# A gated scan on TensorE: small matmul groups joined across heads

## The reference, cut to what matters

```python
A = einsum('bhtd,bhsd,bhtsd->bhts', qc, kc, exp(b_t - b_s))   # t >= s
o = einsum('bhts,bhsv->bhtv', A, vc) + einsum('bhtd,bhdv->bhtv', qc * exp(b), S)
S = exp(b_last) * S + einsum('bhsd,bhsv->bhdv', kc * exp(b_last - b), vc)
```

## Time and profile before

| | |
|---|---|
| median of three runs | 1440.71 us |
| the profiled execution | 1440.95 us |
| its span | 1439.2 us |
| TensorE busy | 1422.2 us, 99% |
| VectorE busy | 873.3 us, 61% |
| ScalarE busy | 573.9 us, 40% |

### The profile page before, as it was taken

One profiled execution on the slowest core, in us unless ns is written; L12 is line 12 of the kernel. 1 busy time (PEld: TensorE's weight loads), 2 busy tenths in 40 slices (PEclk: granted clock), 3 DMA queues, 4 the chain that ended last, 5 costly groups with the idle time before them and its releaser, 6 DMA issues.

```text
span 1439.2 us, 20231 instructions
## 1 busy us (share of the span) xinstructions
PE 1422.2 (99%) x8048; PEld 1176.2 (82%) x8048; DVE 873.3 (61%) x1720; ACT 573.9 (40%) x1076; POOL 0.2 (0%) x4
## 2 busy tenths in 40 slices
PE   8999999999999999999999999999999999999998
PEld 6888888888888888888888888888787787787786
DVE  8887776543333335756467434423788888888655
ACT  6423345423232324533232333423455454555441
POOL 0000000000000000000000000000000000000000
PEclk9999999999999999999999999999999999999999
DMA  9656441352222224023232323222222222222221
GB/s 344 221 197 238 150 158 46 126 198 101 91 100 103 88 102 147 30 103 103 88 103 88 109 97 118 87 89 88 74 74 74 74 74 74 74 74 74 74 73 59
DMA packets 43726, 157.88 MB, mean 110 GB/s; under 512 B 4849, under 2 KB 5233, under 8 KB 43633
## 3 DMA queue, kind: packets, MB, share of 16 engines
q1 hardware_dynamic: 43344, 156.39, 30.9%
q10 hardware_dynamic: 288, 0.21, 0.0%
HBM read 154.48 MB, written 2.10 MB: 109 GB/s over the span
## 4 chain that ended last, share of the span: by engine, by line
PE 97%; DVE 2%; ACT 1%; issue 0%; DMA 0%; ACTq 0%; DVEq 0%
PE PS L503 30%; PE PS L505 29%; PE PS L504 29%; PE PS L898 1%; PE PS L499 1%; PE PS L902 1%; PE PS L892 1%; PE PS L653 1%; PE PS L917 1%; PE PS L844 0%; PE PS L878 0%; PE PS L857 0%; DMA CST<-in_cst 0%; PE PS L886 0%; PE PS L868 0%
## 5 line engine op out<-in xcount | busy, mean ns | idle before, releaser
L503 PE MATMUL PS<-HH,WH 128*128 128x512 f32 (+1 forms) x1072 | 424.1, 396 | 0.0
L505 PE MATMUL PS<-HH,WL 128*128 128x512 f32 (+1 forms) x1072 | 412.0, 384 | 0.0
L504 PE MATMUL PS<-HL,WH 128*128 128x512 f32 (+1 forms) x1072 | 411.3, 384 | 0.0
L1049 DVE TENSOR_TENSOR WL<-RAW,WH 128x1024 fp32r<-128x1024 f32 x217 | 263.9, 1220 | 70.9 <-ACT WH L1765 70.6
L1765 ACT ACTIVATE WH<-RAW 128x1024 fp32r<-128x1024 f32 x217 | 228.7, 1056 | 168.4 <-PE PS L505 133.6
L505 PEld LDWEIGHTS PS<-HH,WL 128*128 128x128 f32 x1072 | 201.5, 188 | 41.2
L503 PEld LDWEIGHTS PS<-HH,WH 128*128 128x128 f32 x1072 | 201.7, 188 | 37.3
L504 PEld LDWEIGHTS PS<-HL,WH 128*128 128x128 f32 x1072 | 202.0, 188 | 35.7
L503 PE MATMUL PS<-WH,ZH 128*128 128x512 f32 x400 | 155.9, 390 | 0.0
L504 PE MATMUL PS<-WL,ZH 128*128 128x512 f32 x400 | 155.7, 389 | 0.0
L505 PE MATMUL PS<-WH,ZL 128*128 128x512 f32 x400 | 155.7, 389 | 0.0
(11 more groups left out here) (268 smaller groups left out, 1758.6 us busy)
## 6 DMA issues: line engine op xcount, KB each, us to landing
RAW<-in_w_fc SPq DMA_DIRECT2D x64, 512.0 KB, 3.2
RAW<-in_hgrn_in SPq DMA_DIRECT2D x64, 512.0 KB, 3.2
RAW<-in_ada SPq DMA_DIRECT2D x44, 512.0 KB, 4.4
RAW<-in_pool_in SPq DMA_DIRECT2D x40, 512.0 KB, 3.3
RAW<-in_w_in SPq DMA_DIRECT2D x26, 512.0 KB, 5.1
RAW<-in_pool_out SPq DMA_DIRECT2D x16, 512.0 KB, 3.2
RAW<-in_hgrn_out SPq DMA_DIRECT2D x16, 512.0 KB, 3.2
RAW<-in_w_out SPq DMA_DIRECT2D x8, 512.0 KB, 3.7
```

Source lines behind the costliest of these rows:

```text
L503: e.matmul(out, wh, xh, start=first, stop=False)
L504: e.matmul(out, wh, xl, start=False, stop=False)
L505: return e.matmul(out, wl, xh, start=False, stop=last)
L1049: e.tensor_tensor(lo, raw(i), hi.bitcast(F32), ALU.subtract).then_inc(taken.sem, taken(i))
```

## The change

- mixing takes two heads: m, the head before, and o, the one before that (heads 0 to 12; LATE = 13 and on finish within their own time). For m: levels 0, 8 and 16 as one group (small_levels), then level 32. For o: level 64 directly behind that group, the turned keys directly behind m's level 32 in the same bank (columns 0 to 383, level 32 in 384 to 447), states, outputs.
- Level 64 is made of 8 matmuls with 32 stationary columns, no longer 4 with 64.
- The steps at which side work goes on are given for each engine. TensorE: 2, 6, 10, 13; VectorE: 2, 9, 11, 18; ScalarE: 3, 7, 8, 13; longer lists for heads 14, 15 and 16. The norm transposes (turn) have steps of their own on TensorE (1, 6, 7, 10) and VectorE (1, 7, 8, 12).
- The gate product of VectorE is at step 1 of the next head (3 before); head 15's at its own step 23.
- At the start keep_going(14) is keep_going(9), and first_low(0) stands ahead of first_modulation(1, 8).

```diff
-            if h == 15 and L in (16, 32, 64, "kt"):
-                return {16: 3, 32: 4, 64: 3, "kt": 4}[L]
-            return {0: 3, 8: 4, 16: 7, 32: 3, 64: 4, "kt": 7, "ds": 3}[L]
+            if h == 15:
+                return {16: 5, 32: 3, 64: 4, "kt": 3, "ds": 4}[L]
+            return {16: 7, 32: 5, 64: 5 if h < LATE else 7, "kt": 5 if h < LATE else 7, "ds": 4}[L]
+        def turned(h):
+            return (copied.sem, copied.of("kt", h)) if h < LATE else banks.taken(("kt", h))
+        def old(h):
+            return h - 2 if 2 <= h <= LATE + 1 else None
...
-            keep_going(14)
+            keep_going(9)
...
                 k0, q1 = halves(t.k, 32)[0], halves(t.q, 32)[1]
                 for i in range(8):
-                    r, c = 32 * (i % 4), 32 * (i // 4)
+                    r, c = 32 * (i % 4), 384 + 32 * (i // 4)
                     m = e.matmul(PS[b][r:r + 32, c:c + 32], k0[:, i, :], q1[:, i, :], start=True, stop=True)
+                if keys is not None:
+                    e.wait_ge(scaled.sem, scaled.of(keys, 128))
+                    for c in blocks[0:3]:
+                        m = e.transpose(PS[b][:, c], Head(keys).k[:, c], IDN)
...
                 k0, q1 = halves(t.k, 64)[0], halves(t.q, 64)[1]
                 for i in range(4):
-                    r, c = 64 * (i % 2), 64 * (i // 2)
-                    m = e.matmul(PS[b][r:r + 64, c:c + 64], k0[:, i, :], q1[:, i, :], start=True, stop=True)
+                    for a in range(2):
+                        r, c = 64 * (i % 2) + 32 * a, 64 * (i // 2)
+                        m = e.matmul(PS[b][r:r + 32, c:c + 64], k0[:, i, 32 * a:32 * a + 32], q1[:, i, :],
+                                     start=True, stop=True)
...
+            def states(h):
+                b = level_bank(h, "ds")
+                claim(b)
+                e.wait_ge(*turned(h))
...
+            def mixing(m, o):
+                small_levels(m)
+                if o is not None:
+                    level_64(o)
                 yield
+                level_32(m, o)
+                yield
+                if o is not None:
+                    states(o)
+                    yield
+                if m >= LATE:
+                    level_64(m)
+                    yield
+                if o is not None:
+                    outputs(o)
+                    yield
...
-                    if n in SIDE or h == 16 and n != 2:
+                    if n in (range(3, 10) if h == 16 else (2, 5, 8, 11, 14, 17) if h == 15 else
+                             (2, 6, 10, 12, 14, 16, 18, 22) if h == 14 else (2, 6, 10, 13)):
                         next(side, None)
+                    if n in ((1, 6, 7, 10) if h < 15 else (1, 11, 12, 14)):
                         next(turn, None)
                     if n == 0 and h:
-                        side = mixing(h - 1)
+                        side = mixing(h - 1, old(h))
...
             for f in range(8):
+                if f == 1:
+                    first_low(0)
                 first_modulation(f, 8)
-                if f:
+                if f > 1:
                     first_low(f - 1)
...
-                    if n == (0 if h == 16 else 3) and gates:
+                    if n in (1, 23 if h == 15 else 1) and gates:
                         gates.pop()()
...
+                    if n in (range(3, 8) if h == 16 else (2, 5, 9, 15, 20) if h == 15 else
+                             (2, 9, 11, 13, 18, 20, 23) if h == 14 else (2, 9, 11, 18)):
                         next(side, None)
+                    if n in ((1, 7, 8, 12) if h < 15 else (1, 12, 13, 16)):
                         next(turn, None)
...
             def last_keys(h):
                 b = level_bank(h, "kt")
                 e.wait_ge(*banks.made(("kt", h)))
-                e.activation(KT, PS[b][:, 0:384], ACT.Copy).then_inc(banks.free[b], 1)
+                m = e.activation(KT, PS[b][:, 0:384], ACT.Copy)
+                if h < LATE:
+                    m.then_inc(copied.sem, copied("kt", h))
...
+            def mixing(m, o):
+                if o is not None:
+                    level_64(o)
+                    yield
+                    last_keys(o)
+                    yield
+                level_32(m)
+                yield
...
+                    if n in (range(3, 7) if h == 16 else (6, 9, 13, 18) if h == 15 else
+                             (3, 7, 8, 12, 14, 17, 22) if h == 14 else (3, 7, 8, 13)):
+                        next(side, None)
                     if n in SIDE or h == 16:
-                        next(side, None)
                         next(turn, None)
```

More of the change, by code:

```diff
@@ L285, in build @@
         SIDE = (1, 3, 6, 9, 12, 15, 18, 20, 22, 23)
+        LATE = 13
         def flat(i):
@@ L832, in project, with small_levels @@
                 yield from column(("hg", h), 2, None, "last" if h == 15 else None)
-            def mixing(h):
+            blocks = [slice(128 * i, 128 * i + 128) for i in range(4)]
+            def small_levels(h):
                 t = Head(h)
-                blocks = [slice(128 * i, 128 * i + 128) for i in range(4)]
                 claim(3)
@@ L848, in mixing @@
                 m.then_inc(banks.full[4], banks.fill(("level", h, 8), 4))
-                yield
                 b = level_bank(h, 16)
@@ L859, in mixing, with level_32 @@
                 m.then_inc(banks.full[b], banks.fill(("level", h, 16), b))
-                yield
-                b = level_bank(h, 32)
+            def level_32(h, keys):
+                t, b = Head(h), level_bank(h, 32)
                 claim(b)
+                if b == 3:
+                    e.wait_ge(*banks.taken(("level", h, 8)))
                 e.wait_ge(scaled.sem, scaled.of(h, 32))
@@ L887, in mixing, with outputs @@
                 m.then_inc(banks.full[b], banks.fill(("kt", h), b))
-                yield
-                claim(3)
-                e.wait_ge(*banks.taken(("kt", h)))
+            def states(h):
+                b = level_bank(h, "ds")
+                claim(b)
+                e.wait_ge(*turned(h))
                 for c in blocks[0:3]:
-                    m = e.matmul(PS[3][:, c], KT[:, c], Z[:, h, c], start=True, stop=True)
-                m.then_inc(banks.full[3], banks.fill(("ds", h), 3))
-                yield
+                    m = e.matmul(PS[b][:, c], KT[:, c], Z[:, h, c], start=True, stop=True)
+                m.then_inc(banks.full[b], banks.fill(("ds", h), b))
+            def outputs(h):
+                t = Head(h)
                 claim(OB)
@@ L1627, in mixing, with states @@
                     pair[:, :, 32:48].rearrange("p g (n l) -> p g n l", l=8)).then_inc(banks.free[4], 1)
[L1628 to L1648, removed]
+                e.wait_ge(*banks.made(("level", h, 16)))
+                e.wait_ge(*banks.taken(("level", h, 8)))
+                e.copy_predicated(
+                    t.diag.rearrange("p i (n a l) -> p i n a l", a=2, l=16)[:, :, :, 1, :],
+                    MSK[:, 768:1024].rearrange("p (i n l) -> p i n l", i=4, l=16),
+                    PS[b][:, 0:256].rearrange("p (i n l) -> p i n l", i=4, l=16)).then_inc(banks.free[b], 1)
+            def states(h):
+                t, b = Head(h), level_bank(h, "ds")
                 e.wait_ge(own.sem, own.of("tot", h, 128))
                 e.wait_ge(*banks.made(("ds", h)))
-                e.tensor_copy(ST[:, 0:128], PS[3][:, 0:128]).then_inc(own.sem, own())
+                e.tensor_copy(ST[:, 0:128], PS[b][:, 0:128]).then_inc(own.sem, own())
                 for i in (1, 2):
@@ L1656, in mixing, with norm_factors @@
                                                in0=ST[:, 128 * i - 128:128 * i], scalar=t.tot[128][:, i:i + 1],
-                                               in1=PS[3][:, 128 * i:128 * i + 128], op0=ALU.mult, op1=ALU.add)
+                                               in1=PS[b][:, 128 * i:128 * i + 128], op0=ALU.mult, op1=ALU.add)
                     if i == 1:
                         m.then_inc(own.sem, own())
-                m.then_inc(banks.free[3], 1)
-                yield
-                yield
+                m.then_inc(banks.free[b], 1)
+            def norm_factors(h):
                 if h % 2:
@@ L1670, in mixing @@
                     norms.append(two_norms(h - 1))
-                yield
+            def mixing(m, o):
+                if o is not None:
+                    scale(o, 64)
+                scale(m, 16)
+                small_levels(m)
+                yield
+                scale(m, 32)
+                yield
+                if o is not None:
+                    states(o)
+                    yield
+                if m >= LATE:
+                    scale(m, 64)
+                    yield
+                if o is not None:
+                    norm_factors(o)
+                    yield
+                if m >= LATE:
+                    states(m)
+                    yield
+                    norm_factors(m)
+                    yield
```

(21 more changed lines are left out.)

57 lines of the change are left out of this document (34 added, 23 removed).

## The result

The changed kernel takes 1446.92 us (median of five, 1446.62 to 1448.02), the kernel before 1440.88 us beside it (1440.66 to 1441.46): a ratio of 1.0043, interval 1.0031 to 1.0055. It is slower by 6.0 us, 0.4%; forecast were 1445.5 and a range of 1438 to 1450. The profiled execution took 1447.41 us, its span is 1445.6 us, 6.4 more than before.

The account below looks back on a forecast made before the run. It took TensorE, 99% busy, as the bound. From 1440.95 us profiled, -9.6 - 0.7 + 0.6 + 13.7 + 0.5 - 0.6 + 0.9 = +4.8 gave 1445.75, less 0.24 for the median: 1445.5, range 1438 to 1450.

Parts of the forecast that it names:

- Joined visits: TensorE's scan: 29 fewer visits from full width to narrow tiles and back, 0.33 us each, -9.6 us.
- Keys behind level 32, norm transposes moved: TensorE's scan: turned keys directly behind level 32 save 0.7 us; norm transposes, losing their cover, cost 0.6.
- The wait for the keys: TensorE's state matmuls wait for ScalarE's KT copy behind forget: 13 times 1.05 us, +13.7, bounds 11.7 to 15.6.
- VectorE: Same operations in other places, no cost; prepare's last operation 0.9 us early with the keys wait, about 0.1 late without.
- 0.1 late without the wait: VectorE's last operation of prepare comes about 0.1 us late per head if the state matmuls don't wait for KT.
- rival A: State matmuls don't wait for KT: 1431.8 us, or 1433 with VectorE 0.1 us late a head; chance 0.14.
- Last heads: Head 14's level 64 late by some 0.3 us, keys finding bank 7 freed about then: +0.5 us, 0 to 1.5.
- The gate product's wait: Head 15's gate product moves to step 23, so TensorE's 0.6 us wait for it goes: -0.6 us.
- Start: VectorE idles for HH(0), shifting all behind it; TensorE has no slack: +0.9 us, bounds -0.3 and +1.0.
- the wait for the keys 13 times: Sign of being right: TensorE waits for ScalarE's KT copy 13 times, near 1.0 us each, 12 to 15 in sum.
- joined groups of 1.25: Sign of being right: joined groups of 1.1 to 1.2 us in place of 0.68 + 0.57 + 0.59.
- second values at 24.38: Sign of being right: a wait of 2 us before the second values at 23.8.

Follow-up runs that it names:

- states-one-later kernel: Changed kernel with TensorE's state matmuls of the older head at step 11 instead of 10, outputs at 14 instead of 13; 1436.32 us.
- keys first: Changed kernel with ScalarE's copy of the turned keys at step 6 instead of 7, ahead of forget; 1432.99 us, ratio 0.9943 to the kernel before.
- old start: Changed kernel with its start as before: keep_going(14), and first_low(0) behind first_modulation(1, 8); 1446.03 us.
- keys first and the old start: Changed kernel with ScalarE's keys copy at step 6, ahead of forget, and the start as before the change; 1431.02 us, ratio 0.9929 to the kernel before.
- new start alone: Kernel before with only keep_going(9) and first_low(0) ahead of first_modulation(1, 8); 1443.12 us, ratio 1.0013.
- keep_going alone: Kernel before with keep_going(9) in place of keep_going(14), VectorE's order as it was; 1442.17 us, ratio 1.0007.

## Why the prediction was right, point by point

The forecast was +4.8 on a profiled run; measured were +6.4 between the spans of the profiles and +6.0 between the medians. Each term, in the prediction's own numbering:

1. **Joined visits.** The mechanism held and the total too, -9.6 forecast. By groups it is 13 x -0.58 and 3 x -0.29 = -8.4. The rest lies in the large matmuls behind them: outside the groups and the wait for the gate product, what the scan's large matmuls take over 0.227 each fell from 2.8 to 1.5 us in sum, 1.3 for the 42 groups that went (29 here, 13 of part 2), 0.03 each. The 29 are then worth -9.3. The term was mis-sized inside: a visit is 0.28 to 0.305, not 0.33. The prediction got 0.31 to 0.36 by taking 0.027 a round off a group. With the visit at 0.29, level 16's eight rounds must cost (0.574 - 0.29) / 8 = 0.036 each.
2. **Keys behind level 32, norm transposes moved.** -0.7 and +0.6 forecast. Measured: 1104.05 - 1102.85 - 0.454 = 0.746 (median 0.742) against 0.461 + 0.341 apart, 13 x -0.06 = -0.8; the norm transposes cost 0.44 behind full-width groups (1.181 less 0.742), as said.
3. **The wait for the keys.** +13.7 forecast, 14.9 by groups, inside the bounds. The step that was mis-sized is the 0.1 us for what a wait costs beside itself: the prediction's gap of 0.96 was right to 0.05 (0.91 listed), but the group is 1.15 dearer. It is 0.24 that is lost beside the listed wait, in all 13 heads and again in the seven of the states-one-later kernel. That is why 1.15 a head was measured and 1.05 forecast. The experiment with the keys first shows the cause: one line's order on ScalarE, 13.9 us.
4. **VectorE.** Nothing forecast, nothing found. But the "0.1 late without the wait", which rival A carried as 1.3 us, wasn't found: with the keys first no joined group waits, and with the old start as well one of the 13 is 0.10 dearer than the others (1.354), with no wait listed. Rival A's other number, 1431.8, was 0.8 above what the kernel with keys first and the old start took, and 1.2 below keys first alone.
5. **Last heads.** +0.5 forecast (0 to 1.5), +0.9 measured: 0.72 at the L909 group (1.495 against 0.78), 0.18 at one L899 group. These are the two places that the prediction named, level 64 of head 14 and its keys, which wait for bank 7; their sizes were the wrong way round. The small one starts at 1330.83, behind the end of VectorE's scaling at 1330.68, where 1330.64 would have been its place; whether norm_factors(13) made that late wasn't tried. The large one was given no price, since the bank was to be free at about the same moment. What holds the bank is ScalarE, whose turn and forget stand in front of the copy of level 64: without the turn there, that group costs 0.77. The gate product's wait is gone, as forecast; its size was the listed 0.6, and by the starts around it, it had cost 0.86 (1345.75 - 1344.77 = 0.98 and 1346.08 - 1345.75 = 0.33 in the trace of before, less 2 x 0.227).
6. **Start.** +0.9 forecast, between 0.9 (in the changed kernel) and 2.0 (before, and with the keys first) by the medians. VectorE's half was right to a tenth: +0.87 alone, by the 0.77 us idle. What was missing is the other half. The prediction took the five fewer matmuls for something that only HL hides; alone they cost +1.0 in the median. What the profiles show of it is a weight tile that lands later near 110 us, for 0.66 us in that kernel's own; the start itself they don't delay (last section). In the profile of after VectorE waited 2.40 for that tile and TensorE did not, so all of its 1.4 us is at the start: some 0.86 is VectorE's order, and 0.56 is the ones-matmuls, which end later in this execution because the clock rises later.

Sum of the scan by the measured terms: -8.4 - 1.3 - 0.8 + 0.6 + 14.9 + 0.9 - 0.9 = +5.0, as read from the starts; with 1.4 at the start it is the 6.4 between the profiles. Of the 1.6 that the forecast was short, 1.2 are the wait's, 0.4 the last heads' and 0.5 the start's, less 0.3 for the gate product and 0.2 for the joined visits. Three of the signs that it named came out beside their marks for the same reasons: the wait for the keys 13 times, but 0.91 each and 11.8 in sum where 1.0 and 12 to 15 were said, joined groups of 1.25 where 1.1 to 1.2 were, and second values at 24.38 where 23.8 was.

## What to carry to other kernels

When a dependent operation is moved closer to its producer, write out for each engine what stands in its queue ahead of the copy in between, evictions that belong to the main loop included: here one operation moved by one step on an engine that is 40% busy was worth 13.9 us, more than all the joining. Size a wait of TensorE by what the group costs from large start to large start, not by the listed wait: it was some 0.25 us more here. Size a join likewise, with the matmuls further behind counted in. And test a small rider (here three lines at the start) by itself over many runs: it cost 1 to 2 us of what the rest could give.

## What the runs showed that was not expected

**Less at the start, more at 110 us.** The profiles of all kernels with keep_going(9) have the in_ada tile late: VectorE's wait is 2.40 (after), 3.33 (keys first), 3.93 (states later), 4.40 (new start alone) and 3.10 (keep_going alone), and TensorE waits 0.4 to 1.6 us for what follows in the last four; with keep_going(14) it is 1.01 to 1.63, and TensorE doesn't wait. VectorE starts on the tile at 108.3 to 110.5 us with nine and at 105.7 to 106.7 with 14. What in 1.2 us of matmuls that nobody reads moves a load 90 us later by 2 to 4 us wasn't found: the loads' order is the same, and no run here changes the loads alone. It stays open.

**The ones-matmuls.** Two matmuls of 128x512 at 9.3 us, four entries, take between 1.98 and 3.49 us over the kernels, with no wait listed and nothing changed ahead of them. The first three rows are from the kernel with keys first, the last from that with the old start.

```profile
6.70 2.93 PE L664 MATMUL PS<-CST 128*128 128x128 f32 x12 [6.70 <-DMA CST<-in_cst]
9.42 1.98 PE L701 MATMUL PS<-Z,ONES 128*128 128x512 f32 x4
11.23 3.73 PE L664 MATMUL PS<-CST 128*128 128x128 f32 x32
```

```profile
9.41 3.49 PE L701 MATMUL PS<-Z,ONES 128*128 128x512 f32 x4
```

The cause can be read from the rows beside them. Ahead of the ones-matmuls the entries of keep_going take about 0.23 us each (2.72 us for 12), behind them 0.12 (3.73 for 32): TensorE goes from the lower of its two clock levels (1.2 GHz) to the higher (2.4 GHz) somewhere in between. The trace's record of the granted clock begins, at the higher level, at 9.61 us with keys first and at 12.64 with the old start; for the time ahead of it there is no record, and the table by stretch prints 1.00 there all the same. In before it is 11.17, in after 12.30. Over the 12 profiles it lies between 9.61 and 12.64 with the new start and with the old one alike, though TensorE is busy from 6.6 to 6.8 us on in all of them. What sets the moment is not shown.

It does move the start. With VectorE's old order the second values begin at 22.8 to 23.2 us where the clock rises by 11.4 us, and at 23.6 and 23.7 where it rises at 12.4 and 12.6; with the new order at 23.8 to 23.9 where it rises by 11.3, and at 24.4 where it rises at 12.2 and 12.3. keep_going(9) or (14) makes no difference to this. Of a single profile's start, then, more than half a microsecond is chance, which is why the start was judged by the medians of many runs.

**What a wait costs beside itself.** 0.24 us for each wait of the L917 group, whether the listed wait is 0.91 or 0.24. It is not this group's alone: over two starts, the wait for the gate product in before (0.59 listed) cost 0.86, and the four near 110 us (0.39, 0.46, 1.38 and 1.56 listed) cost 0.27 more each. It is no rule either: two waits of 0.43 at 242 and 597 us, in every profile, cost 0.48. The profile's table of weight loads lists 16.9 us for the 13 of after, 1.3 each, so the weights of the group are not loaded while it waits; that this is what the 0.24 is made of was not tried.
